# Feed-forward up projection by seven half-size products for each pair of tiles

## The reference, cut to what matters

```python
def conv_ffn(xn, w_up, conv_w, conv_b, w_down):      # xn (1, 512, 1024), w_up (1024, 2 * 2816)
    a, b = jnp.split(xn @ w_up, 2, axis=-1)
    a = lax.conv_general_dilated(a, conv_w[:, None, :], (1,), [(2, 0)], ...,
                                 feature_group_count=2816) + conv_b      # causal, width 3, per channel
    return (jax.nn.silu(a) * b) @ w_down

h = h + conv_ffn(rms_norm_2(h, norm_ffn), ffn_up, ffn_conv, ffn_conv_b, ffn_down)
```

## Time and profile before

| | us |
|---|---|
| three runs, median | 2037.79 |
| profiled execution, span from first to last instruction | 2032.0 |
| TensorE matmuls busy | 1960.2 |
| VectorE busy | 1128.5 |
| ScalarE busy | 801.2 |
| GpSimd busy | 448.7 |

### The profile page before, as it was taken

How to read it: one execution, slowest core, us unless ns; L and a number is a source line. 1 busy time by engine, 2 the same in 40 slices (tenths; PEclk the granted TensorE clock), 3 DMA queues, 4 the chain that set the end, 5 groups by cost and what they waited for, 6 DMA issues and landing times.

```text
span 2032.0 us, 31665 instructions
## 1 busy us (share of the span) xinstructions
PE 1960.2 (96%) x13058; PEld 1526.4 (75%) x13058; DVE 1128.5 (56%) x1810; ACT 801.2 (39%) x1369; POOL 448.7 (22%) x537
## 2 busy tenths in 40 slices
PE   8999999999999988889999999999999999999999
PEld 6857888888766778767787854568887778888887
DVE  5354444444577856759356765545365556666432
ACT  4274332232546532344225376653254442232211
POOL 0551000000403566743000056622230010000000
PEclk9999999999999989999999999999999999999999
DMA  5203222222224210002384100032232222222322
GB/s 181 88 23 102 93 94 94 93 94 94 95 95 150 83 64 4 4 13 86 104 222 160 63 22 1 1 125 94 83 126 82 73 87 100 94 94 93 95 87 88
DMA packets 46733, 174.91 MB, mean 86 GB/s; under 512 B 5071, under 2 KB 5455, under 8 KB 45824
## 3 DMA queue, kind: packets, MB, share of 16 engines
q1 hardware_dynamic: 43488, 154.35, 23.0%
q0 software_dynamic: 3104, 18.56, 2.8%
HBM read 166.53 MB, written 10.55 MB: 87 GB/s over the span
## 4 chain that ended last, share of the span: by engine, by line
PE 88%; DVE 4%; ACT 4%; POOL 2%; issue 1%; DMA 0%; SPq 0%; DVEq 0%; POOLq 0%; ACTq 0%
PE ps L300 23%; PE ps L301 22%; PE ps L305 22%; PE ps L2723 3%; PE ps L1435 2%; PE ps L1012 2%; PE ps L2731 2%; PE ps L1419 1%; PE ps L1711 1%; ACT arena L1540 1%; PE ps L1388 1%; DVE arena L1499 1%; PE ps L1868 1%; PE ps L2076 1%; PE ps L3430 1%
## 5 line engine op out<-in xcount | busy, mean ns | idle before, releaser
L280 ACT ACTIVATE w_hi<-wring 128x1024 fp32r<-128x1024 f32 (+1 forms) x267 | 280.1, 1050 | 574.4 <-PE ps L305 552.7
L286 DVE TENSOR_TENSOR w_lo<-wring,w_hi 128x1024 fp32r<-128x1024 f32 (+1 forms) x267 | 331.7, 1243 | 203.5 <-ACT w_hi L280 201.2
L300 PE MATMUL ps<-ffn_input_hi,w_hi 128*128 128x512 f32 x352 | 139.5, 396 | 0.0
L301 PE MATMUL ps<-ffn_input_hi,w_lo 128*128 128x512 f32 x352 | 139.1, 395 | 0.0
L1589 POOL TENSOR_TENSOR arena<-arena 128x512 f32<-128x512 f32 (+3 forms) x160 | 112.5, 727 | 28.0 <-DVE arena L1491 23.0
L300 PE MATMUL ps<-gate_input_hi,w_hi 128*128 128x512 f32 x256 | 106.0, 414 | 4.1 <-DVE w_lo L286 2.5
L300 PE MATMUL ps<-mlp_input_hi,w_hi 128*128 128x512 f32 x256 | 101.6, 397 | 0.0
L300 PE MATMUL ps<-mlp_hi,w_hi 128*128 128x512 f32 x256 | 101.2, 395 | 0.0
L301 PE MATMUL ps<-gate_input_hi,w_lo 128*128 128x512 f32 x256 | 101.2, 395 | 0.0
L301 PE MATMUL ps<-mlp_input_hi,w_lo 128*128 128x512 f32 x256 | 101.2, 395 | 0.0
L301 PE MATMUL ps<-mlp_hi,w_lo 128*128 128x512 f32 x256 | 101.2, 395 | 0.0
(11 more groups left out here) (485 smaller groups left out, 4556.4 us busy)
## 6 DMA issues: line engine op xcount, KB each, us to landing
wring<-weights SPq DMA_DIRECT2D x276, 512.0 KB, 3.5
bias_wide_scratch<-bias_line_scratch POOLq DMA_DIRECT2D x1, 4096.0 KB, 27.3
arena<-bias_wide_scratch POOLq DMA_DIRECT2D x1, 4096.0 KB, 18.5
wring<-weights SPq DMA_DIRECT2D x9, 384.0 KB, 3.1
arena<-x_t SPq DMA_DIRECT2D x4, 512.0 KB, 7.4
xn_scratch<-arena POOLq DMA_DIRECT2D x1, 2048.0 KB, 6.8
x_scratch<-arena POOLq DMA_DIRECT2D x1, 2048.0 KB, 9.6
arena<-xn_scratch POOLq DMA_DIRECT2D x1, 2048.0 KB, 9.4
```

The costliest lines, as they stand in the source:

```text
L280: act.activation(self.w_hi[:, m % SPLIT, 0:n], self.wring[:, g % RING, 0:n], ACT.Copy).then_inc(self.w_hi_ready, 1)
L286: dve.tensor_tensor(self.w_lo[:, m % SPLIT, 0:n], self.wring[:, g % RING, 0:n], self.w_hi[:, m % SPLIT, 0:n].bitcast(F32), ALU.subtract).t ...
L300: pe.matmul(out, hi[:, c, :], src.hi[:, at + c, :], start=(at + c == 0), stop=False)
L301: pe.matmul(out, lo[:, c, :], src.hi[:, at + c, :], start=False, stop=False)
```

## The change

A pair of units (tile a above, tile b below; input features 0 to 511 left, 512 to 1023 right) is taken as a 2x2 block matrix of quarters 128x512, the input as 2x2 blocks of 512 features by 256 tokens. Seven products in Winograd's form of Strassen's method replace eight. Their weights are the four quarters (one of them, s3, written over quarter 21) and the sums s1, s2, s4; their inputs are the four blocks and T1 to T4, differences of blocks, which GpSimd makes once, ahead of the stage. Each product is 12 matmuls of 128x128 by 256 columns.

GpSimd makes the four sums of the next pair, one pair ahead (`sums`), and in pairs 2 to 11 one hidden low part (`pool_step`). ScalarE makes seven high parts of 512 columns per pair, three products ahead, copies three partial results out of PSUM (`copy`), and takes over the first convolution step (`begin_conv`). VectorE makes all seven low parts (`BY_POOL` is empty), adds the partial results (left, right, below), and does the scaling, convolution, gate and the output in two halves for the pair before. The two weight buffers of 1024 columns become four halves; a half is used again once its product is done. Hidden tiles 0 to 9 get their high and low parts during the stage, 10 to 21 their low parts on VectorE behind it. Semaphores of several stages become shared with a base count (`Signal`), which changes no instruction's place.

```diff
+    def convert_lo(self, eng, m):
+        self.wait_hi_ready(eng, m)
+        eng.tensor_tensor(self.w_part(self.w_lo, m), self.split_source(m), self.w_part(self.w_hi, m).bitcast(F32),
+                          ALU.subtract).then_inc(self.split[m].lo[0], 1)
...
+class WinogradInput(DeferredNorm):
...
+    def scalar(self, act):
+        j = DT_ - 1
+        self.scale(act, j)
+        self.high(act, j, 0)
+        self.pair0.first_sums_high(act)
+        self.high(act, j, 1)
+        self.square(act, j)
+        self.high(act, j, 2)
+        self.k.act_tables(act, LN_EXP)
...
+class Winograd(SplitStage):
...
+    PARTS = (("11", B11), ("12", B21), ("s2", T2), ("s1", T1), ("s3", T3), ("s4", B22), ("22", T4))
+    N, AHEAD = 7, 3
+    BY_POOL = ()
...
+    def open_banks(self, pe, n, i):
+        k = self.k
+        if i == 0:
+            if n >= 2:
+                self.corner.wait(pe, n - 1)
+            else:
+                k.wait_acc_drained(pe, self.acc0 - 2 + n)
...
+                if i in (2, 4, 5):
+                    self.copied.wait(pe, 3 * n + {2: 1, 4: 2, 5: 3}[i])
+                if i == 6:
+                    self.below.wait(pe, n + 1)
+                out = self.side_bank(n, i != 1) if i in (1, 3, 5) else self.corner_bank(n)
+                first = i in (0, 1, 3)
+                u = self.ops[self.N * n + i]
+                k.wait_lo_ready(pe, u)
+                hi, lo = (k.w_part(w, u).rearrange("p (c m) -> p c m", m=P) for w in (k.w_hi, k.w_lo))
+                for c in range(4):
...
+                mm.then_inc(self.part.sem, 1)
+                if n == 0 and i == 2:
+                    self.xs.mean(pe)
...
+        self.wait_raw(pool, n)
+        if n:
+            k.wait_lo_ready(pool, self.ops[self.N * n - 4])
+        pool.tensor_tensor(s1, a21, a22, ALU.add).then_inc(self.summed.sem, 1)
+        if n:
+            k.wait_lo_ready(pool, self.ops[self.N * n - 5])
+        self.summed.wait(pool, 4 * n + 1)
+        pool.tensor_tensor(s2, s1, a11, ALU.subtract).then_inc(self.summed.sem, 1)
+        pool.tensor_tensor(a21, a11, a21, ALU.subtract).then_inc(self.summed.sem, 1)
+        if n:
+            k.wait_lo_ready(pool, self.ops[self.N * n - 2])
+        self.summed.wait(pool, 4 * n + 2)
+        pool.tensor_tensor(s4, a12, s2, ALU.subtract).then_inc(self.summed.sem, 1)
+    def gpsimd(self, pool):
+        for n in range(self.pairs):
+            if n + 1 < self.pairs:
+                self.sums(pool, n + 1)
+            self.pool_step(pool, n)
...
+    def copy(self, act, n, i):
+        dst = {0: 0, 2: 1, 3: 2}[i]
+        src = self.side_bank(n, 1) if i == 3 else self.corner_bank(n)
+        if n:
+            (self.left, self.right, self.below)[dst].wait(act, n)
+        self.part.wait(act, self.N * n + i + 1)
+        act.activation(self.copied_to[:, dst], src, ACT.Copy).then_inc(self.copied.sem, 1)
+    def scalar(self, act):
+        k = self.k
+        for n in range(self.pairs):
+            for i in range(self.N):
+                g = self.N * n + i + self.AHEAD
+                if g < len(self.ops):
+                    k.convert_hi(act, self.ops[g])
+                elif g == len(self.ops) + self.AHEAD - 1:
+                    k.convert_hi(act, self.then.us[0][0])
+                self.scalar_step(act, n, i)
+                if i in (0, 2, 3):
+                    self.copy(act, n, i)
+        self.scalar_end(act)
...
+        self.vector_begin(dve)
+        for n in range(self.pairs):
+            for i in range(self.N):
+                if i == 2:
+                    self.part.wait(dve, self.N * n + 2)
+                    self.copied.wait(dve, 3 * n + 1)
+                    dve.tensor_tensor(self.left_dst(dve, n), self.side_bank(n, 0), self.copied_to[:, 0], ALU.add).then_inc(self.left.sem, 1)
+                if i == 5:
+                    self.part.wait(dve, self.N * n + 5)
+                    self.copied.wait(dve, 3 * n + 3)
+                    dve.tensor_tensor(self.below_dst(dve, n), self.corner_bank(n), self.copied_to[:, 2], ALU.add).then_inc(self.below.sem, 1)
+                if i == 6:
+                    self.part.wait(dve, self.N * n + 6)
+                    dve.tensor_tensor(self.right_dst(dve, n), self.side_bank(n, 1), self.copied_to[:, 1], ALU.add).then_inc(self.right.sem, 1)
+                g = self.N * n + i + self.AHEAD
+                if g < len(self.ops):
+                    if g % self.N not in self.BY_POOL:
+                        k.convert_lo(dve, self.ops[g])
+                elif g == len(self.ops) + self.AHEAD - 1:
+                    k.convert_lo(dve, self.then.us[0][0])
+                self.vector_step(dve, n, i)
+        self.vector_end(dve)
...
+class ConvFfn(Winograd):
...
+    def pool_step(self, pool, n):
+        if 0 <= n - 2 < self.FIRST:
+            self.hidden_lo(pool, n - 2)
...
+    def scalar_step(self, act, n, i):
+        if n == 0 and i == 3:
+            self.xs.guess(act)
+        if n and i == 0:
+            self.begin_conv(act, n - 1)
+        if i == 1 and 0 <= n - 2 < self.FIRST:
+            self.hidden_hi(act, n - 2)
+        if n and i == 3:
+            self.tanh(act, n - 1)
+        if n == self.pairs - 1 and i >= 3:
+            for j in range(self.FIRST + 2 * (i - 3), self.FIRST + 2 * (i - 2)):
+                self.hidden_hi(act, j)
...
+        if step == 1:
+            dve.wait_ge(self.begun_conv, m + 1)
+            k.after_dve(dve, dve.scalar_tensor_tensor(c, a[:, 1:1 + S], k.vec("conv", FT2 + m), c, ALU.mult, ALU.add))
...
+    def out(self, dve, m):
+        c = self.t0[:, m % 2, :]
+        self.part.wait(dve, self.N * m + 7)
+        dve.scalar_tensor_tensor(self.hidden[:, m, 0:HALF_S], c[:, 0:HALF_S], 0.5, self.corner_bank(m), ALU.mult,
+                                 ALU.mult).then_inc(self.out_ready, 1)
+        dve.wait_ge(self.out_ready, 2 * m + 1)
+        dve.nop().then_inc(self.corner.sem, 1)
+        self.below.wait(dve, m + 1)
+        dve.scalar_tensor_tensor(self.hidden[:, m, HALF_S:S], c[:, HALF_S:S], 0.5, self.below_dst(dve, m), ALU.mult,
+                                 ALU.mult).then_inc(self.out_ready, 1)
...
+    def vector_step(self, dve, n, i):
...
+            if i == 0:
+                self.scale(dve, m)
+            if i in (1, 2):
+                self.conv(dve, m, i)
+            if i == 4:
+                self.gate(dve, m)
+            if i == 6:
+                self.out(dve, m)
...
+    def vector_end(self, dve):
+        last = self.pairs - 1
+        self.scale(dve, last)
+        self.k.convert_lo(dve, self.then.us[0][1])
+        self.conv(dve, last, 1)
+        self.conv(dve, last, 2)
+        for j in range(self.FIRST, last - 3):
+            self.hidden_lo(dve, j)
+        self.gate(dve, last)
+        self.out(dve, last)
+        for j in range(last - 3, FT2):
+            self.hidden_lo(dve, j)
+        self.k.convert_lo(dve, self.then.us[0][2])
```

More of the change, by code:

```diff
@@ L51 @@
 SPLIT = 2
+HALF_UNIT = 512
+HALVES = 2 * SPLIT
 NA, NX = 3, 5
@@ L164, in take_unit, with take_halves @@
         return len(self.units) - 1
+    def take_halves(self, n):
+        if n == 2:
+            self.half += self.half % 2
+        at = self.half % HALVES
+        before = sorted({self.half_user[h] for h in range(at, at + n) if h in self.half_user})
+        for h in range(at, at + n):
+            self.half_user[h] = len(self.split)
+        self.half = (at + n) % HALVES
+        return at, before
     def take_split(self, acc, n=UNIT, last=True):
@@ L340, in gpsimd, with place @@
         pass
+    def place(self, j):
+        return j
 class InverseRoot:
@@ L1015, in wait_weights @@
         k, unit = self.k, self.us[i][0]
-        pe.wait_ge(k.w_lo_ready if low else k.w_hi_ready, unit + 1)
+        if low:
+            k.wait_lo_ready(pe, unit)
+        else:
+            k.wait_hi_ready(pe, unit)
     def unit(self, pe, i, low):
@@ L1358, in __init__ @@
                 pairs += units[f].last
+        self.s_full = Signal(k, "scores_full", NT * len(units))
+        self.s_drained = Signal(k, "scores_drained", 2 * NT * len(units))
+        self.p_ready = Signal(k, "probs_ready", NT * len(units))
+        self.inv_ready = Signal(k, "inverse_ready", NT * len(units))
+        if units[0].gate is not None:
+            self.gated = k.sem("inverse_gated")
+        self.scaled = Signal(k, "probs_scaled", 2 * NT * len(units))
+        self.t_full = [Signal(k, f"probs_t_full{e}", self.t_count[e]) for e in range(2)]
+        self.t_drained = [Signal(k, f"probs_t_drained{e}", self.t_count[e]) for e in range(2)]
+        self.pv_done = Signal(k, "values_done", len(units))
+        self.out_drained = Signal(k, "out_drained", pairs)
     def place_t(self, key, e):
@@ L1366, in wait_out @@
     def wait_out(self, eng, pair):
-        eng.wait_ge(self.out_drained, pair + 1)
+        self.out_drained.wait(eng, pair + 1)
     def score_bank(self, e, i):
@@ L3539, in __init__ @@
+class ConvFfn(Winograd):
```

(38 more changed lines are left out.)

457 lines of the change are left out of this document (310 added, 147 removed).

## The result

The changed kernel takes 2128.07 us (median; 2125.85 to 2131.17) against 2038.01 us before (2035.96 to 2043.05): ratio 1.0439 [1.0415, 1.0463], 90 us slower. The forecast was 2096 us, with a range up to 2122: the direction is right, the size is not, and the time lies 6 us above the range. The profiled execution took 2129.08 us, 1.9 above its span.

A forecast was written before the change was run, and what follows sets the result against it. TensorE's matmul spacing bounds the kernel before. Up projection and the wait behind it: 18.5 + 13.1 + 10 x 14.2 + 9 x 13.1 + 10.5 + 3.4 = 305.4 us against 247.3, +58: span 2090, time 2096 us, range 2050 to 2122.

The forecast's parts named there:

- pair 0: First pair of the up projection: 18.5 us, with product 2 waiting for ScalarE's corner copy until 6.9 us after the start.
- the walk: One pair of the up projection, instructions in order of time: 13.1 us, 14.2 with hidden low part, 10.5 without GpSimd's turns.
- the prediction's nothing: Cross output ahead of the stage: extra small helper instructions per tile counted as no time, bounds 0 and 3 us.
- the 5.8 us: Runs' median lies 5.8 us above the profiled span; with it the span forecast of 2090 becomes 2096 us.
- TensorE's side: Up projection: 1056 matmuls of 512 columns become 1848 of 256, 0.1186 us each; alone -28 us.
- GpSimd's turns: Up projection: GpSimd's sums and hidden low parts alternate with VectorE's instructions reading two SBUF operands; each turn costs VectorE 1.07 us.
- Rival 1: Up projection: the turns cost nothing, GpSimd's sums fall into VectorE's waits; -9, 2029 us; chance 0.10.
- rival 2: Up projection: only the port's capacity counts, 11.5 us a pair, VectorE's other waits hidden; +26, 2064 us; chance 0.17.
- rival 4: Up projection: TensorE's clock falls; quarter of stage at 1.2 GHz +34, all of it +136 us or more; chance 0.05.
- Behind the stage: After the up projection: VectorE still owes low parts, so TensorE waits 3.4 us for the third unit's low part.
- The signs announced: Profile after: TensorE idle before products 0, 5, 6, released by VectorE; low parts at 1.7 us; idle behind ScalarE would refute.

The follow-up runs named there:

- experiment 7: Kernel before the change with every matmul of the up projection cut in two of 256 columns: 2043.11 us, ratio 1.0031.
- experiment 1: Changed kernel with the four weight sums of every pair left out, GpSimd only signalling: 2072.8 us, ratio 1.0174 to the kernel before.
- experiment 2: Changed kernel with the weight sums made by VectorE instead of GpSimd from pair 1 on: 2088.39 us, ratio 1.0248 to the kernel before.
- Experiment 8: Changed kernel, sums and hidden low parts on VectorE, pair 0's sums early, three corner banks, ScalarE's convolution step behind high part 4: 2076.06 us, ratio 1.0202.
- experiment 6: Changed kernel with pair 0's four sums on GpSimd ahead of input tile 4 instead of tile 7: 2128.26 us, ratio 1.0457 to the kernel before.
- experiment 5: Changed kernel with filler matmuls into a spare bank ahead of TensorE's waits: 2119.78 us, ratio 1.0414 to the kernel before.
- Experiment 4: Changed kernel with ScalarE's third copy of a pair issued ahead of the tanh: 2133.02 us, ratio 1.0476 to the kernel before.

## Why the forecast was too low

The forecast for the span was 2090, measured are 2127.2. The 37 us are: pair 0 +7.4, pair 1 +1.2, pairs 2 to 11 +12.3, pairs 12 to 20 +6.1 (5.5 by the walk, the rest in pair 12, which begins at the 1.2 GHz level, and in pair 14), pair 21 +1.1, what lies behind the stage +3.8, and +5.2 ahead of the stage. Of these 5.2 the cross output, which prepares the new input, has nothing (45.3 us before and after, so the prediction's nothing held there); they lie ahead of it, in code that the change does not touch, and in the traces of the eight other kernels the cross output starts anywhere from 1613.4 to 1623.1 us. By size the walk comes first, with some 13 us in pairs 1 to 20, then pair 0 with 7.4, then the clock with 6. So the steps that failed are the start of the walk, the head of pair 0 and the clock left out of the sum; each is taken up below. On the other side the 5.8 us that I put between the span and the time were 1.9.

- **TensorE's side: right.** 1848 matmuls 0.119 us apart inside a product, behind pair 0 with no wait between them, and experiment 7 for the width by itself.
- **GpSimd's turns: right as the larger cause.** Experiments 1 and 2 show it: 2128 becomes 2073 without the sums and 2088 with the sums on VectorE. The price of a turn was right too: 1.02 to 1.08 us (the two low parts at 1907.23 have 2.36 where two alone have 1.28; the convolution step at 1903.82 has 1.02 over its 0.75). The turn at low part 4 cost 0.78, since the second sum began ahead of it. Rival 1 falls with this, and rival 2 with the 13.7 us of a steady pair, where it had 11.5. The 7.3 us of instructions with two SBUF inputs that it uses add up to 7.4 from the prediction's own prices.
- **The walk: 13.1, measured 13.7.** From the end of the first output half, by the timeline of pair 15: low part 3 starts at 0.65 (the walk: 0.4), the scaling ends at 1.94 (1.6), high part 4 at 3.59 (3.2), low part 4 at 5.0 (4.5), the second convolution step at 8.4 (7.85), the first half at 13.7 (13.1). Over half of the error is there once the scaling has ended. The first output half costs 0.56 to the next start, with the wait for its own increment behind it, and the second 0.50; the walk had 0.4 for the second, and the list of prices 0.33 and 0.46. The 0.50 is no price of the output half: low part 3 starts 0.03 us behind the end of ScalarE's high part 3 (1898.80 plus 0.63), which waits for TensorE's product 6 of the pair before. Experiment 8 has 0.34 in that place (1858.48 to 1858.82). I sized the chain nearly right and its start wrong, and left high part 3 out of it. The extra us of the hidden low part came as forecast (14.8 against 13.7 where the clock stays up).
- **What stands behind the turns: wrong.** Without turns the walk had 10.5; experiment 1 has 11.8. I did not see that ScalarE, tanh then copy then high part, would then hold low part 0 of the next pair. Two errors of opposite sign (1.3 too low without turns, turns 0.7 too dear) left one of 0.6, so that the walk came so near is partly luck.
- **Pair 0: 18.5, measured 25.9, the largest miss in one pair.** The failed step is the copy at 6.9 us after the start: the prediction names ScalarE's own instructions behind the last input tile and puts what they wait for at nothing. Product 2, which needs that copy, started at 13.5. I placed the four sums behind the input and had nothing for them ahead of it. They stand ahead of tile 7 in GpSimd's order, and GpSimd also makes tile 7's differences: 6 us of sums (1664.17 to 1670.2) while VectorE's three low parts of tile 6 took 4.38 us. Moving the sums gives 2.7 of the 7.4 back (experiment 6), leaving them out 3.5 (experiment 1, pair 0 at 22.3). The rest is there without them, and in experiment 6 it stands in ScalarE's waits of 1.44 and 1.05 us for low parts and for GpSimd's differences. TensorE works at the 1.2 GHz level for 13.7 us of the pair (the 12 matmuls of product 2 start within 2.51 us in place of 1.31), but that costs little: with half of that time gone, pair 0 is 0.2 us shorter (experiment 5).
- **The clock: rival 4, held too small and held apart.** It had 0.05 as a case of its own with a quarter of the stage. In truth it comes on top of the forecast: 51 of 330 us of the stage at 1.2 GHz, and 6 us by experiment 5 in pairs 1 to 12. The trace shows the way by which it gets into the pair. In pairs 4, 6, 8, 9 and 11, where 4.9 to 5.8 us are at the low level, product 6 ends late, high part 3 behind it, and low part 3 of the next pair starts 1.5 to 1.7 us behind the second output half in place of 0.5. Those five add up to 5.9 us. A wait of 2.59 with a clock of 0.66 behind it stood in the earlier trace rows, and my own walk had TensorE idle for over 3 us in each pair.
- **Behind the stage: 3.4, measured 5.5 of waits.** TensorE's two waits there, the second for the third unit's low part as forecast:

```profile
1994.09 0.47 PE L375 MATMUL ps<-ffn_hi,w_hi 128*128 128x512 f32 x1 [1.20 <-issue]
...
2009.78 0.80 PE L375 MATMUL ps<-ffn_hi,w_hi 128*128 128x512 f32 x1 [4.25 <-DVE w_lo L361]
```

  The rest of the +7 goes with a granted clock of 0.98 there.
- **The signs announced.** TensorE's waits before products 0 (0.22 us), 5 and 6, stretched low parts, PSUM sums unchanged, pairs 2 to 11 one us longer: seen. "Released by VectorE" and "VectorE's idle small" were half right. The largest of the three waits is put down to ScalarE, which the prediction had named as a sign that it is wrong, and VectorE has 1.7 us of waits a pair. Experiment 4 shows that for product 5 the name in the bracket was not the cause.

Left open: whether a mixture of plain pairs and pairs of seven products, which would need the input in both forms at once, beats the kernel before. It was not tried. TensorE's two waits of 1.8 us a pair in pairs 2 to 11 were left as they are, and so was what is left of pair 0's head.

## What to carry to other kernels

Fewer matmuls are worth nothing where the helpers' work per product grows: here TensorE's need fell from 11.2 to 10.0 us a pair, and VectorE's rose from 7.1 to 11.3 with the sums. Put that sum ahead of any work on the order. Short two-operand sums belong on VectorE, into a wait that it has anyway, if they cost it 0.6 each there and 1.05 each as turns from GpSimd. In a walk, price the start of the chain (output halves with increments between them, and the other engine's instruction that the next one needs) as closely as its links. At the first pair, count what each helper waits for, and not only what it does. Where TensorE will wait twice in a pair for 1.8 us, add the clock to the forecast, not beside it.
